# Moving small steps between engines in a one-core decoder kernel: an earlier state update, earlier layer-norm sums, and three reordered queues

## What is computed

```
h, (C, n, m) = mlstm_mixer(x, w_in, b_gate, w_out, C0, n0, m0)
x = layer_norm(ALPHA * x + h, ln_g[0, 0], ln_b[0, 0])
x = layer_norm(ALPHA * x + square(relu(x @ w_up)) @ w_down, ln_g[0, 1], ln_b[0, 1])
k, v = split(x @ w_kv);  q = x @ w_q
x = layer_norm(ALPHA * x + attend(q, ctx) @ w_out_b, ln_g[1, 0], ln_b[1, 0])
x = layer_norm(ALPHA * x + mlp(x), ln_g[1, 1], ln_b[1, 1])
C_new = ae * C + einsum('bhs,bhsd,bhsv->bhdv', ws, k, v)     # the memory state, an output
```

## Time and profile before

| | |
|---|---|
| time, median of 3 executions | 911.21 us (909.43 to 915.8) |
| the profiled execution: its time | 909.43 us |
| its span in the trace | 907.6 us |
| PE busy | 897.9 us, 99% of the span |
| DVE, ACT, POOL busy | 622.3, 438.1 and 64.7 us |
| share of PE in the chain that ended last | 96% |

### The profile page before, as it was taken

How to read it: one execution, slowest core, us unless ns; L and a number is a source line. 1 busy time by engine, 2 the same in 40 slices (tenths; PEclk the granted TensorE clock), 3 DMA queues, 4 the chain that set the end, 5 groups by cost and what they waited for, 6 DMA issues and landing times.

```text
span 907.6 us, 18748 instructions
## 1 busy us (share of the span) xinstructions
PE 897.9 (99%) x7491; PEld 838.6 (92%) x7491; DVE 622.3 (69%) x1089; ACT 438.1 (48%) x826; POOL 64.7 (7%) x81
## 2 busy tenths in 40 slices
PE   9999999999999999999999999999999999999996
PEld 8999988999999999999888778987999999999975
DVE  6487668788976575676676847446568797747536
ACT  5445666476355363545344453355547634536321
POOL 0010006400000000330000000000230000000000
PEclk9999999999999999999999999999999999999999
DMA  9972215754454445457988997998945455544401
GB/s 287 269 248 93 94 48 139 204 180 149 148 169 141 140 155 165 169 199 244 323 300 292 355 370 289 398 400 342 290 140 170 156 159 181 154 157 140 139 1 59
DMA packets 132331, 182.78 MB, mean 201 GB/s; under 512 B 5875, under 2 KB 113211, under 8 KB 132244
## 3 DMA queue, kind: packets, MB, share of 16 engines
q1 hardware_dynamic: 126938, 177.56, 58.9%
q0 software_dynamic: 640, 2.10, 0.9%
q10 hardware_dynamic: 4666, 1.92, 0.8%
HBM read 175.24 MB, written 6.32 MB: 200 GB/s over the span
## 4 chain that ended last, share of the span: by engine, by line
PE 96%; DMA 2%; ACT 1%; DVE 1%; issue 0%; SPq 0%; DVEq 0%; POOL 0%; POOLq 0%
PE ps L624 24%; PE ps L626 23%; PE ps L625 23%; PE ps L1013 7%; PE ps L1055 4%; PE ps L1113 2%; DMA page<-in_cache_v_dram 2%; PE ps L902 1%; PE ps L904 1%; PE ps L903 1%; PE ps L638 1%; PE ps L655 1%; PE ps L741 0%; PE ps L808 0%; PE ps L911 0%; PE ps L913 0%
## 5 line engine op out<-in xcount | busy, mean ns | idle before, releaser
L1217 ACT ACTIVATE w_hi<-raw 128x1024 fp32r<-128x1024 f32 x192 | 202.4, 1057 | 227.4 <-PE ps L626 204.4
L1619 DVE TENSOR_TENSOR w_lo<-raw,w_hi 128x1024 fp32r<-128x1024 f32 x192 | 237.4, 1240 | 102.2 <-ACT w_hi L1217 102.1
L624 PE MATMUL ps<-x_hi,w_hi 128*128 128x322 f32 (+1 forms) x888 | 278.8, 314 | 0.0
L626 PE MATMUL ps<-x_hi,w_lo 128*128 128x322 f32 (+1 forms) x888 | 275.6, 310 | 0.0
L625 PE MATMUL ps<-x_lo,w_hi 128*128 128x322 f32 (+1 forms) x888 | 275.2, 310 | 0.0
L624 PEld LDWEIGHTS ps<-x_hi,w_hi 128*128 128x128 f32 x888 | 167.3, 188 | 5.2 <-ACT k_turned L1508 2.9
L624 PE MATMUL ps<-h_hi,w_hi 128*128 128x320 f32 x552 | 170.9, 310 | 0.0
L626 PE MATMUL ps<-h_hi,w_lo 128*128 128x320 f32 x552 | 170.3, 309 | 0.0
L625 PE MATMUL ps<-h_lo,w_hi 128*128 128x320 f32 x552 | 170.3, 308 | 0.0
L625 PEld LDWEIGHTS ps<-x_lo,w_hi 128*128 128x128 f32 x888 | 167.9, 189 | 0.2
L626 PEld LDWEIGHTS ps<-x_hi,w_lo 128*128 128x128 f32 x888 | 166.9, 188 | 0.0
(11 more groups left out here) (345 smaller groups left out, 985.8 us busy)
## 6 DMA issues: line engine op xcount, KB each, us to landing
raw<-in_w_up_dram SPq DMA_DIRECT2D x32, 1024.0 KB, 5.8
raw<-in_w_down_dram SPq DMA_DIRECT2D x32, 1024.0 KB, 5.2
page<-in_cache_k_dram SPq DMA_DIRECT2D x64, 512.0 KB, 5.7
page<-in_cache_v_dram SPq DMA_DIRECT2D x64, 512.0 KB, 9.3
raw<-in_w_in_a_dram SPq DMA_DIRECT2D x11, 1024.0 KB, 8.8
raw<-in_w_kv_dram SPq DMA_DIRECT2D x8, 1024.0 KB, 6.5
raw<-in_w_out_a_dram SPq DMA_DIRECT2D x4, 1024.0 KB, 5.5
raw<-in_w_q_b_dram SPq DMA_DIRECT2D x4, 1024.0 KB, 5.6
```

Of the source, the lines that this page charges most:

```text
L624: mm(out, WH[PLACE[t]][:, k, :], hi[:, k, 0:width], start=(k == 0), stop=False)
L626: last = mm(out, WL[PLACE[t]][:, k, :], hi[:, k, 0:width], start=False, stop=(k == 7))
L1217: A(WH[PLACE[t]][:, :, :], raw_tile(t), ACT.Copy)\
L1619: V.tensor_tensor(WL[PLACE[t]][:, :, :], raw_tile(t), WH[PLACE[t]][:, :, :].bitcast(F32), ALU.subtract)\
```

## The change

1. PE: the four state steps with matmuls (2 to 5) each move one tile earlier. `state_step(2)` stands right behind tile 1 of `Q_WOA`, the following ones behind tiles 2, 3 and 4.
2. PE: in `ln_stats` the two matmuls on the sums stand ahead of chunk 3 of the second tile, not of chunk 5, in all three layer norms.
3. DVE: the `w_lo` split of tile 10 moves from behind the copies of the turned rows to ahead of them.
4. DVE: in the last tile of `Q_WOA` (n = 7) the split of a weight tile comes ahead of `x_low(0, 7)` and no longer behind it. For n below 7 the second `split_to` had nothing left to do, and nothing changes.
5. DVE: `out_low(0, ...)` is done in pass 5 of the loop over the prompt's heads and no longer in pass 6.
6. POOL: the three instructions of the key sum move from ahead of `sums(0, 1)` to behind `sums(0, 4)`.

```diff
@@ PE, heads_out and the loop over Q_WOA
                     last = chunk(1, k)
                 last.then_inc(s_mm, 1)
+                state_step(2)
...
             for n in range(2, 8):
                 dense(8 * Q_WOA + n, HH[0], HL[0])
-                state_step(n)
+                state_step(n + 1)
@@ PE, ln_stats
-                    if k == 5:
+                    if k == 3:
@@ DVE, around the turned rows
-            for n in range(7):
+            for n in range(8):
                 split_to(8 * Q_QK + n + 3)
             dve.wait_ge(s_lnt, 1)
...
-            split_to(8 * Q_QK + 10)
             dve.wait_ge(s_c0, 16 * 8)
@@ DVE, the loop over Q_WOA
-                if n < 7:
-                    split_to(t + 3)
+                split_to(t + 3)
                 x_low(0, n)
-                split_to(t + 3)
@@ DVE, the prompt's heads
-                if i == 6:
+                if i == 5:
                     out_low(0, 0)
                     out_low(0, 1)
@@ POOL
-            pool.wait_ge(s_wk, 8)
-            own(G.tensor_tensor(Wst[:, :], wsK[:, 0, :], wsK[:, 1, :], ALU.add))
-            own(G.tensor_copy(wsK[64:128, 2, :], Wst[0:64, :]))
-            G.tensor_tensor(wsK[64:128, 2, :], wsK[64:128, 2, :], Wst[64:128, :], ALU.add).then_inc(s_ws2, 1)
-            pool.wait_ge(s_ws2, 1)
             for n in range(1, 8):
                 sums(0, n)
+                if n == 4:
+                    pool.wait_ge(s_wk, 8)
...
+                    pool.wait_ge(s_ws2, 1)
```

More of the change, by code:

```diff
@@ L2246, in _ @@
             pool.wait_ge(s_wid, 1)
-            pool.wait_ge(s_wk, 8)
-            own(G.tensor_tensor(Wst[:, :], wsK[:, 0, :], wsK[:, 1, :], ALU.add))
-            own(G.tensor_copy(wsK[64:128, 2, :], Wst[0:64, :]))
-            G.tensor_tensor(wsK[64:128, 2, :], wsK[64:128, 2, :], Wst[64:128, :], ALU.add).then_inc(s_ws2, 1)
-            pool.wait_ge(s_ws2, 1)
             for n in range(1, 8):
                 sums(0, n)
+                if n == 4:
+                    pool.wait_ge(s_wk, 8)
+                    own(G.tensor_tensor(Wst[:, :], wsK[:, 0, :], wsK[:, 1, :], ALU.add))
+                    own(G.tensor_copy(wsK[64:128, 2, :], Wst[0:64, :]))
+                    G.tensor_tensor(wsK[64:128, 2, :], wsK[64:128, 2, :], Wst[64:128, :], ALU.add).then_inc(s_ws2, 1)
+                    pool.wait_ge(s_ws2, 1)
             for j in range(4):
```

## The result

| | before | after |
|---|---|---|
| median of 20 runs, us | 910.07 | 915.64 |
| lowest and highest, us | 908.8, 915.8 | 912.03, 917.37 |
| profiled execution, us | 909.43 | 915.77 |
| its span, us | 907.6 | 914.0 |
| its mean granted clock | 0.998 | 0.995 |

The ratio is 1.0055, with a 95% interval of 1.0044 to 1.0066; it compares the executions as a whole, and the two medians alone have a ratio of 1.0061. The kernel has become slower by about 0.55%, which is 5.6 us in the medians and 6.4 us between the two profiled spans. That is under 1%, but clear of no change, since the interval does not reach 1.

What follows compares the result with a forecast made beforehand. PE, 99% busy, was taken as the bound. Edits 1 to 6 summed as 1.5 + 0 + 0.15 + 0.15 + 0 + 0.05 = +1.85 us, on the median 911.21 giving 913.1 us; bounds 912.4 to 915.8, range 909.5 to 916.5.

Steps and rivals of the forecast that it cites:

- main term: Edit 1, behind tile 1 of Q_WOA: PE waits for the weighted keys at the first state product, 1.5 us.
- the rival of the clock: PE's first long wait in the body lowers its clock: 2.4 us more, 915.5 us, chance 0.06.
- The later steps: State steps behind tile 3 and later, needing DVE's C update: costed at 0, up to 0.6 us in all.
- the slack of 0.3 us: Before a later state step, DVE needs 4.4 us up to its C update while PE works 4.7 us.
- the key sum takes its 0.3 us from another split: Edit 6: POOL's moved key sum slows a later DVE split by 0.3 us, leaving DVE's total loss unchanged.
- fills that hole: Edit 4, last Q_WOA tile: the 1.22 us split fills x_low's 1.06 us wait for ACT, overrunning about 0.15 us; hidden, 0 us.
- POOL is late: Key sum and three pairs of sums stretch a third beside DVE: 3.2 us wait at the cast, 916.3 us, chance 0.08.
- The waits that go: In Q_WOA, ACT's 3.71 us for POOL and DVE's 2.52 us for ACT go, with no gain for PE.
- a wait of 1.5 us is under half of those 3.3 us: Against a clock fall: at the trace's end the clock fell only about 3.3 us after PE's last matmul.
- Its price: Cost of a clock fall, 2.4 us: the program's 17 first matmuls took 4.90 us against 2.55 us.

Runs made afterwards that it cites:

- the key sum behind the third sums: The kernel after with POOL's key sum behind the third pair of sums, not the fourth: 913.87 us, ratio 1.0050 to the kernel before.
- edit 1 with ready operands: The kernel before with edit 1, DVE's state(1) ahead of the Q_WOA loop and ACT's masked(0) ahead of its first split: 910.81 us, ratio 1.0010.
- the spread turns: The kernel before with thin matmuls moved behind tiles 0 and 1 of Q_O and the ln_cols wait ahead of tile 6: 910.28 us, ratio 1.0000.
- the two kernels with ready steps: The kernel before with edit 1 and its operands made ready first, without edit 6 (910.81 us) and with it (910.70 us).
- the ten fillers: The kernel after with ten extra matmuls, product thrown away, ahead of state step 2: 914.76 us, ratio 1.0040 to the kernel before.
- both fillers: The kernel after with ten extra matmuls ahead of state step 2 and five ahead of Q_O's first tile: 916.03 us, ratio 1.0065 to before.
- the two other versions of after: The kernel after without edit 4 (914.79 us, ratio 1.0043), and with the key sum behind the third sums (913.87 us, ratio 1.0050).
- the ready steps with edit 6: The kernel before with edit 1, its operands made ready first, and edit 6: 910.70 us, ratio 1.0006.

## Why the prediction was right or wrong

The forecast of a small loss within 1% was right, its main term is the largest wait in the trace, and the median lies in its range. That 915.64 lies there is in part luck: +1.85 us were worked out, while the spans differ by 6.4 and the medians by 5.6. The range held because it was wide and because it started from a median of three executions, 911.21, which was 1.1 us above that of twenty. The waits alone add up to 3.33 us, inside the bounds for them; the rest is the rival of the clock.

1. **Edit 1** is as worked out: 1.48 us for 1.5, on `wsk`, between the last matmul of tile 1 and tile 2.
2. **The later steps** cost 0, as put down, but not for the reason given. Without edit 6 the slack of 0.3 us does not hold: edit 1 alone waits 0.73 us. The bound allowed for a split of 1.53 us beside the key sum and for no longer `x_low`; with edit 1 alone the two took 1.88 and 1.16 us, beside POOL's first sums. Edit 6 moves this work apart.
3. **Edit 3** was sized 0.15 and measured 0.67 us in after and, with edit 3 alone, 1.68 us between starts (a wait of 1.62). The copies end as late as the landing makes them, and both the landing (41.69, 41.93 and 42.42 us) and PE's arrival move between executions. One landing time was taken as fixed.
4. **Edits 2, 4 and 6** were sized 0.15 and measured 1.18 us. The step that failed is "the key sum takes its 0.3 us from another split". It hit a split and an `x_low`, and `x_low` is not stretched by a quarter but to three times its time; POOL's later sums then stretched the last split and the last `x_low` too. The cover was overrated as well: edit 1 takes the last step (1.09 us) out from between tile 5 and tile 7, so that PE reaches the next tile a microsecond sooner after the stretched `x_low`. Alone these edits wait 0.16 us; in after, where edit 1 is present, 0.39 + 0.47. That the split "fills that hole" (edit 4) failed with it: in after DVE did not wait for ACT there. The rival "POOL is late" came in a small size, and by its own mechanism. The key sum took 4.18 us (158.31 to 162.49) where 6.05 were put down, but the last pair but one took 3.1 us, where before it took 2.1, and the last (2.7 us in both kernels) could start only behind it. PE waited 0.47 us for that.
5. **Edit 5** was put at 0.05, and is 0.02 us in the run with it alone.
6. **The waits that go** (ACT's 3.71, DVE's 2.52 us) did go and gave nothing, since PE had no idle time there before.
7. **The clock**, 3.08 of the 6.41 us, was the rival with a chance of 0.06. The step that failed is its dismissal: "a wait of 1.5 us is under half of those 3.3 us", which took the program's end, where the clock stayed up for 3.3 us after the last matmul, as the measure for a wait in the body. In the body the clock fell behind waits of 0.60 and 1.32 us, and without any wait. Its price, 2.4 us from the start of the program, was too high for one fall (1.54), too low for the two that occurred. Nor is that row a reading at the lower level: the profile's clock column says 1.00 over those 17 matmuls, though they start 0.28 us apart. In the falls the column says 0.50 and the starts are 0.27 us apart.

What the 14 traces show of the falls in the body: in tile 2 of `Q_WOA`, two of the four kernels in which step 2 waits 1.3 us (after, and the key sum behind the third sums), none of the ten in which it does not. At the turn to `Q_O` or up to 1.6 us into the tile behind it, two of the four with a wait on `ln_cols`, four of the nine without one, and not in the kernel that spreads the thin matmuls. Near 10 us, where all the kernels are alike, four of the 14. So at `Q_O` no wait is needed, and that the thin matmuls bring the fall is not shown; in tile 2 the wait looks necessary and is not sufficient, on one trace for each kernel.

The times agree. Subtract the waits in the trace from the median and before's cheapest 908.6 us: after keeps 3.7 us, edit 1 alone 2.1, edit 1 with ready operands 1.4, and before itself 1.5 to 2.3. So the kernel after pays about one fall more than before in a typical execution.

The mean granted clock of every execution says the same. Before's profiled execution has 0.998 with no fall in the body, after's 0.995 with two. Executions at 0.998 or more are 23 of 80 for the kernel before, 7 of 12 with edits 2, 4 and 6, 7 of 12 with the spread turns, 2 of 12 with edit 1 alone, none of 12 with edit 3 alone, 8 of 22 in the two kernels with ready steps, 4 of 12 with the ten fillers, 2 of 8 with both fillers, none of 17 in the two other versions of after, and 1 of 24 for after. That one took 912.03 us, where before's cheapest and the 3.33 us of waits make 911.9. This points to the wait of edit 3 as a second reason for more falls, though a fall at `Q_O` doesn't need it. How the extra fall divides between the two places, and what decides in which execution it comes, is open; more traces of the same kernel would tell.

The Trainium skill, page "GPSIMD Engine Reference", section "Specifications", has VectorE instructions with two SBUF inputs contend with GpSimd. The rows of after agree further than the prediction used it: `w_lo` (1.58 us) and `x_low` (1.58) have two such inputs and were stretched, while the update of C at 162.76 and the residual at 166.83, with one input in PSUM, took their usual 2.15 and 0.47 us beside POOL's sums.

None of the versions tried beats the kernel before: edits 2, 4 and 6 alone (0.9993), the spread turns (1.0000) and the ready steps with edit 6 (1.0006) all have 1 in their interval.

## What to carry to other kernels

When the bounding engine is 99% busy, idle time on the others is no reserve, and a new order can only add waits: look for the operand that each moved instruction meets first, and ask whether its time is a landing that moves from run to run. Price a new wait of TensorE with a possible clock fall on top (1.54 us here), and read matmul starts and the clock column, since the busy share shows neither. An instruction with two SBUF inputs on GpSimd should not be put beside the VectorE instructions that TensorE is about to wait for, and edits that are free one by one should be costed together, since each one's cover may be the other's.

## What the runs showed of the hardware

- TensorE's clock fell to half for about 3.4 us in the middle of dense work, in some executions of a kernel and not in others. No idle time ahead of it was needed (the runs with edits 2, 4 and 6 and with both fillers), and a wait of 1.32 us did not always bring it (edit 1 alone). One fall cost 1.54 us.
- VectorE's `x_low` (128 x 320) took 0.55 us alone and 1.58 us beside a 64 x 512 addition on GpSimd, which itself took 2.15 in place of 1.42 us. POOL's sum of squares (128 x 320) took 1.87 us beside a split and an `x_low`, 0.87 us elsewhere.
- GpSimd's key sum over 128 x 512 took 3.00 us as its first `TENSOR_TENSOR` and 1.28 us as a later one; the sum of X that comes first now took 1.23 us, no more than later ones that take 0.88 to 1.31. So the 1.7 us did not pass to the next in line. Whether they are a cost of first use is not shown.
